# A first stage rebuilt around PSUM: the convolution, the samples and the GLA projections of a hybrid decoder step

## The reference

```python
h = rmsnorm(x, norm_mix)
p = h @ w_in                               # 1024 -> 9248 columns
qkv, z, b_a, a_a, q_b, k_b, v_b, r_b, lr, g_a, g_b = split(p)
xc = concat([conv_buf, qkv])               # 3 old rows ahead of the new ones
conv = sum(cw[i] * xc[i:i+T] for i in range(4))
new_buf = last 3 rows of xc
q_a, k_a, v_a = split(silu(conv))          # 8 heads of 128; q_a, k_a are l2-normalized
beta, g = sigmoid(b_a), -exp(a_log) * softplus(a_a + dt_bias)
o_a, S_a = gated_delta_net(S_a, q_a, k_a, v_a, g, beta)
lg = log_sigmoid(lr @ gla_gate_up + gla_gate_bias) / 16
o_b, S_b = gla(S_b, q_b / sqrt(128), k_b, v_b, lg)    # 4 heads, keys 128, values 256
merged = sigmoid(g_a) * (norm(o_a)*silu(z)) @ w_proj_a + sigmoid(g_b) * (norm(o_b)*silu(r_b)) @ w_proj_b
x = x + merged @ w_out
x = x + experts(rmsnorm(x, norm_ffn))      # 32 experts in 4 groups, 2 chosen per token
y = rmsnorm(x, norm_final)
```

## Time and profile before

| | us |
|---|---|
| Median of 3 runs (lowest, highest) | 1073.52 (1070.82, 1075.18) |
| Profiled execution | 1078.4 |
| its span | 1076.7 |
| Busy: PE, PEld, DVE, ACT, POOL | 928.6, 745.7, 442.7, 298.3, 304.9 |
| Mean granted clock of TensorE | 0.895 |

### The profile page before, as it was taken

One profiled execution on the slowest core, in us unless ns is written; L12 is line 12 of the kernel. 1 busy time (PEld: TensorE's weight loads), 2 busy tenths in 40 slices (PEclk: granted clock), 3 DMA queues, 4 the chain that ended last, 5 costly groups with the idle time before them and its releaser, 6 DMA issues. The chain is left out here.

```text
span 1076.7 us, 15504 instructions
## 1 busy us (share of the span) xinstructions
PE 928.6 (86%) x6446; PEld 745.7 (69%) x6446; DVE 442.7 (41%) x718; ACT 298.3 (28%) x602; POOL 304.9 (28%) x281
## 2 busy tenths in 40 slices
PE   4989877988899699968988999999769999889964
PEld 2888757988898698745558999999756455455521
DVE  5689874544313532153355632464142222102213
ACT  3454363231112334211036443432201111110102
POOL 8366446375341200034234301756000000000000
PEclk9999889998688698988868999999955999999996
DMA  9544006000002592300443554420190999999981
GB/s 252 174 141 128 1 1 169 1 1 1 2 1 79 152 299 79 118 0 1 154 163 87 157 157 157 156 79 1 59 422 8 394 420 419 419 420 419 419 370 47
DMA packets 97910, 175.71 MB, mean 163 GB/s; under 512 B 8964, under 2 KB 84324, under 8 KB 85493
## 3 DMA queue, kind: packets, MB, share of 16 engines
q1 hardware_dynamic: 97832, 174.62, 44.9%
HBM read 163.66 MB, written 10.95 MB: 162 GB/s over the span
## 5 line engine op out<-in xcount | busy, mean ns | idle before, releaser
L243 PE MATMUL ps<-rounded,rounded 128*128 128x304 f32 x640 | 201.4, 315 | 13.5 <-DVE rounded L231 9.5
L245 PE MATMUL ps<-rounded,rounded 128*128 128x304 f32 x640 | 195.9, 306 | 0.0
L244 PE MATMUL ps<-hL,rounded 128*128 128x304 f32 x512 | 157.9, 308 | 0.0
L243 PEld LDWEIGHTS ps<-rounded,rounded 128*128 128x128 f32 x640 | 123.5, 193 | 15.7 <-DVE rounded L231 9.7
L231 POOL TENSOR_TENSOR rounded<-ring,rounded 128x2048 fp32r<-128x2048 f32 x21 | 98.3, 4679 | 104.4 <-ACT rounded L225 104.4
L245 PEld LDWEIGHTS ps<-rounded,rounded 128*128 128x128 f32 x640 | 123.6, 193 | 0.0
L225 ACT ACTIVATE rounded<-ring 128x2048 fp32r<-128x2048 f32 x48 | 91.3, 1910 | 37.5 <-PE ps L245 16.0
L244 PEld LDWEIGHTS ps<-hL,rounded 128*128 128x128 f32 x512 | 99.7, 195 | 0.4 <-issue 0.2
L231 DVE TENSOR_TENSOR rounded<-ring,rounded 128x2048 fp32r<-128x2048 f32 x27 | 63.3, 2344 | 70.9 <-ACT rounded L225 70.2
L1904 DVE TENSOR_TENSOR arena<-arena,ps 128x512 f32<-128x512 f32 (+1 forms) x48 | 32.9, 685 | 123.3 <-PE ps L2022 123.3
L1952 PE MATMUL ps<-arena 128*128 128x128 f32 (+1 forms) x384 | 74.7, 328 | 2.5 <-DVE arena L1871 2.5
(11 more groups left out here) (334 smaller groups left out, 1602.4 us busy)
## 6 DMA issues: line engine op xcount, KB each, us to landing
ring<-in_w_in SPq DMA_DIRECT2D x36, 1024.0 KB, 5.7
ring<-in_expert_w_gate SPq DMA_DIRECT2D x32, 1024.0 KB, 14.4
ring<-in_expert_w_up SPq DMA_DIRECT2D x32, 1024.0 KB, 19.6
arena<-in_expert_w_down SPq DMA_DIRECT2D x32, 1024.0 KB, 17.6
arena<-in_state_gla SPq DMA_DIRECT2D x4, 1024.0 KB, 6.7
out_sg_s<-arena SPq DMA_DIRECT2D x4, 1024.0 KB, 4.2
ring<-in_w_proj_a SPq DMA_DIRECT2D x4, 1024.0 KB, 5.4
ring<-in_w_proj_b SPq DMA_DIRECT2D x4, 1024.0 KB, 5.1
```

The lines of the kernel that those rows point to most:

```text
L243: self.nc.tensor.matmul(self.psum[b][:, 0:NT], h[:, j, c], xh(j), start=(j == 0), stop=False)
L244: self.nc.tensor.matmul(self.psum[b][:, 0:NT], h[:, j, c], xl(j), start=False, stop=False)
L245: ins = self.nc.tensor.matmul(self.psum[b][:, 0:NT], lo[:, j, c], xh(j), start=False, stop=(j == KB - 1))
```

## The change

In the first stage:

- GpSimd prepares slot 0 alone, high part and low part, and takes all later low parts up to slot 19 except that of slot 1 (VectorE's). Its masks are built in pieces between them. The transfer of slot 0 goes out right after x, slot 1 ahead of the small columns.
- The high part of the activations moves from VectorE to ScalarE. Block 0 starts with the first piece of the activations that is ready.
- The low-rank product becomes 24 rounded matmuls and goes behind block 1, the gates' turns behind block 2, the log decays behind block 5.
- The convolution of the prompt reads PSUM where the block was made, in four shifted operations; the block's bank is freed by the convolution. There is no XC for the prompt.
- The samples of eight blocks are gathered in a PSUM bank (XS) beside their old rows, put there by a product with the identity for eight blocks at a time (`history`), and convolved together in seven operations (`sample_conv`). `new_buf` is collected by ScalarE.
- GLA's slots follow the convolution, values first (order of `WIN`). Twelve units of `unit_of_slot`, with the sums of squares, norms and turns of the delta heads spread between them by the table AFTER; the squares are ScalarE's, the inverse roots are written to PSUM. Then eight blocks of q_b and k_b, with the turns of the old rows between them.
- The results lie in ring slots 4 to 7 (VB, QKB) until the GLA stage has used them, and with them the two gate tables (UP, GB), loaded at the start of `delta`. From slot 20 on the ring is shifted by four (`slot`, `occupant`, `fills`), so that four slots are loaded during GLA and the next ones in `merge`.

The GLA stage keeps the log gates, the key turns and its loop. It waits for the delta stage's stores later than before: GpSimd at once, VectorE ahead of its first pair, ScalarE at its third exponents.

The core of the diff:

```diff
+def slot(n):
+    return (n if n < N_Z else n + 4) % SLOTS
+
+def occupant(n):
+    return max((m for m in range(n) if slot(m) == slot(n)), default=None)
...
+    def unit_of_slot(self, pe, n, c, b, HI):
+        pe.wait_ge(self.w_lo, n + 1)
+        hi, lo = (w.rearrange("p (j c) -> p j c", j=KB) for w in (HI[n % 3], self.LOW[:, slot(n), :]))
+        o = self.psum[b][0:L[c], 0:256]
+        for j in range(KB):
+            x, y = (h[:, j, T0[c]:T0[c] + L[c]] for h in (self.hH, self.hL))
+            self.nc.tensor.matmul(o, x, hi[:, j, :], start=(j == 0), stop=False)
+            self.nc.tensor.matmul(o, x, lo[:, j, :], start=False, stop=False)
+            ins = self.nc.tensor.matmul(o, y, hi[:, j, :], start=False, stop=(j == KB - 1))
+        ins.then_inc(self.unit_done, 1)
...
+    AFTER = {1: ("ss0",), 2: ("v0", "v1", "ss2"), 3: ("v2", "v3", "ss4"), 4: ("v4", "v5", "ss6"), 5: ("v6", "v7", "ss8"),
+             6: ("k0", "k1", "ss10"), 7: ("k2", "k3", "ss12"), 8: ("k4", "k5", "ss14"), 9: ("k6", "k7")}
...
     @block.gpsimd  (front)
+        k.arrived(pl, 0)
+        nc.gpsimd.tensor_copy(HI[0], k.ring[:, 0, :]).then_inc(k.w_hi, 1)
+        k.low_part(pl, nc.gpsimd, 0, HI)
...
+        pl.drain().then_inc(s["mask_ready"], 1)
+        k.low_part(pl, nc.gpsimd, 2, HI)
+        k.low_part(pl, nc.gpsimd, 3, HI)
         blocks(BLK, 16)
...
+        for n in range(8, N_Z):
+            k.low_part(pl, nc.gpsimd, n, HI)
...
     @block.scalar  (front)
+        for j in range(KB):
+            act.wait_ge(s["xT_done"], j + 1)
+            nc.scalar.activation(hH[:, j, :], psum[4 + j % 4][:, 0:NT], ACT.Copy, scale=nm[:, j:j + 1]).then_inc(s["hH_ready"], 1)
+        k.high_part(act, 2, HI)
...
         for b in range(NCB):
+            g = b // 8
+            if b == 2:
+                low_rank()
             if b == 3:
+                gates_by_token()
+            if b == 4:
+                gate_exps()
+            if b == 7:
                 decays()
...
+            nc.scalar.activation(XS[g][:, b % 8, :, 3:], psum[b % 4][:, TP:NT].rearrange("p (a r) -> p a r", r=TS), ACT.Copy).then_inc(s["xs_ready"], 1)
+            nc.scalar.activation(LAST[:, b, 0:3], psum[b % 4][:, TP - 3:TP], ACT.Copy).then_inc(s["tail_ready"], 1)
+            if b % 8 == 7:
+                act.wait_ge(s["xs_ready"], b + 1)
+                sample_tail(g)
+            if b % 2 and b // 2 + 3 <= N_VB + 2:
                 k.high_part(act, b // 2 + 3, HI)
             if b >= 2:
                 silu(b - 2)
+            if b in (10, 18):
+                sample_silu(b // 8 - 1)
...
+        def square(i):
+            b = KEYS_FIRST[i][1]
+            if i >= 2:
+                act.wait_ge(s["ssum_done"], i - 1)
...
+            nc.scalar.activation(SQ[:, i % 2, :], place(b), ACT.Square).then_inc(s["sq_ready"], 1)
+        def norm(i):
+            act.wait_ge(s["ssum_done"], i + 1)
+            p = psum[5 + 2 * (i % 2)][:, 0:NT]
+            link(nc.scalar.activation(RS[:, i % 2, :], p, ACT.Ln, bias=epsc))
+            nc.scalar.activation(p, RS[:, i % 2, :], ACT.Exp, scale=-0.5).then_inc(s["rs_ready"], 1)
...
     @block.vector  (front)
+        def sample_conv(g):
+            dve.wait_ge(s["last_ready"], g + 1)
...
+            link(nc.vector.tensor_tensor(acc, XS[g][:, :, :, 0:TS], weight(0), ALU.mult))
+            for r in range(1, CW):
+                link(nc.vector.tensor_tensor(tap, XS[g][:, :, :, r:r + TS], weight(r), ALU.mult))
+                ins = nc.vector.tensor_tensor(acc, tap, acc, ALU.add)
...
         for b in range(NCB):
-            dve.wait_ge(s["hist_ready"], b + 1)
-            if b >= 2:
-                dve.wait_ge(s["conv_silu"], b - 1)
-            x, o = XC[:, b % 3, :], CV[:, b % 2, 0:XW - 3]
-            link(nc.vector.tensor_scalar(o, x[:, 0:XW - 3], cw[:, 0, b:b + 1], None, ALU.mult))
+            dve.wait_ge(s["tail_ready"], b + 1)
+            if b >= 3:
+                dve.wait_ge(s["conv_silu"], b - 2)
+            x, o = psum[b % 4], CV[:, b % 3, :]
+            link(nc.vector.tensor_scalar(o, x[:, 0:TP], cw[:, 3, b:b + 1], None, ALU.mult))
             for r in range(1, CW):
-                ins = nc.vector.scalar_tensor_tensor(o, x[:, r:XW - 3 + r], cw[:, r, b:b + 1], o, ALU.mult, ALU.add)
+                ins = nc.vector.scalar_tensor_tensor(o[:, r:], x[:, 0:TP - r], cw[:, 3 - r, b:b + 1], o[:, r:], ALU.mult, ALU.add)
...
+            if b == 2:
+                gates_before()
+            if b == 4:
+                gates_after()
+            if b % 8 == 7:
+                sample_conv(b // 8)
...
     @block.tensor  (front)
         for b in range(NCB):
+            if b >= 4:
+                pe.wait_ge(s["conv_ready"], b - 3)
+            k.block_of_slot(pe, b // 2, b % 2, b % 4, HI, arrives=s["xT_evac"] if b == 0 else None)
...
+            if b == 1:
+                low_rank()
+                pe.wait_ge(s["sc_in"], 16)
                 pe.wait_ge(s["par_ready"], 1)
+                history(0)
+                history(1)
...
+            if b == 5:
+                log_decays()
+            if b == 11:
+                pe.wait_ge(s["acc_ready"], 1)
+                pe.wait_ge(s["last_ready"], 1)
+                history(2)
...
+        for u in range(NV):
+            q, c = divmod(u, 3)
+            n = N_VB + q
+            if u < 4:
+                pe.wait_ge(s["conv_ready"], 21 + u)
+            else:
+                pe.wait_ge(s["vb_ready"], u - 3)
+            k.unit_of_slot(pe, n, c, u % 4, HI)
+            for kind, i in extras(u):
...
+        for b in range(8):
+            pe.wait_ge(s["vb_ready"], NV) if b < 4 else pe.wait_ge(s["qkb_ready"], b - 3)
+            k.block_of_slot(pe, N_QB + b // 2, b % 2, b % 4, HI)
```

More of the change, by code:

```diff
@@ L64, in units, with fills @@
 def units(n):
-    return sum(3 if N_VB <= k < N_Z or k >= N_WO else 2 for k in range(n))
+    return sum(3 if N_VB <= k < N_QB or k >= N_WO else 2 for k in range(n))
+def slot(n):
+    return (n if n < N_Z else n + 4) % SLOTS
+def occupant(n):
+    return max((m for m in range(n) if slot(m) == slot(n)), default=None)
+def fills(n):
+    return sum(slot(m) == slot(n) for m in range(n + 1))
 def named(nc, stage, names):
@@ L198, in load_w @@
     def load_w(self, sp, n):
-        if n >= SLOTS:
-            sp.wait_ge(self.unit_done, units(n - SLOTS + 1))
+        if occupant(n) is not None:
+            sp.wait_ge(self.unit_done, units(occupant(n) + 1))
         if n < N_PA:
@@ new lines, in front @@
+    SC = k.carve(2432, CONV)
+    VT = k.carve(2432, 8 * NT, 8, NT)
+    HI = [k.carve_r(A1 + SW * p, SW) for p in range(3)]
+    CV = k.carve(14720, 3 * TP, 3, TP)
+    SQ = k.carve(15536, 2 * NT, 2, NT)
+    RS = k.carve(16144, 2 * NT, 2, NT)
+    XN = k.carve(17792, 3072, 3, D)
+    SCO = k.carve(17792, CONV)
+    CWR = k.carve(20864, 128)
+    wsm = k.carve(20992, KB * 48, KB, 48)
+    wsH, wsL = (k.carve_r(21376 + KB * 48 * p, KB * 48, KB, 48) for p in range(2))
+    smT = k.carve(22144, NT)
@@ L359, in _ @@
             blocks(GR[:, r, :], m)
+        k.low_part(pl, nc.gpsimd, 5, HI)
+        for r, m in ((3, 32), (4, 16)):
+            v = GR[:, r, :].rearrange("p (a h b) -> p a h b", h=2, b=m)
+            for h, src in ((0, SL), (1, U)):
+                half = src.rearrange("p (a h b) -> p a h b", h=2, b=m)
+                link(nc.gpsimd.tensor_copy(v[:, :, h, :], half[:, :, h, :]))
+            blocks(GR[:, r, :], m)
+        k.low_part(pl, nc.gpsimd, 6, HI)
         link(nc.gpsimd.tensor_tensor(GM[:, 0, :], U, BLK, ALU.mult))
@@ L577, in tr, with history @@
             return nc.tensor.transpose(out, in_, ident[0:n, 0:n])
+        def history(g):
+            for b in range(8 * g, 8 * g + 8):
+                ins = mm(XS[g][:, b % 8, :, 0:3], SC[0:24, 128 * b:128 * b + 128], ident[0:24, 0:24].rearrange("p (a r) -> p a r", r=3),
+                         start=True, stop=True)
+            ins.then_inc(s["hist_done"], 1)
         pe.wait_ge(s["ident_ready"], 1)
@@ L592, in _ @@
-        pe.wait_ge(s["xT_evac"], 8)
-        for j in range(KB):
-            for x in (hH, hL):
-                ins = mm(psum[7][0:48, 200:200 + NT], wsm[:, j, :], x[:, j, :].bitcast(F32),
-                         start=(j == 0 and x is hH), stop=(j == KB - 1 and x is hL))
-        ins.then_inc(s["lr_done"], 1)
-        pe.wait_ge(s["smT_ready"], 1)
-        for c in range(3):
-            tr(psum[6][0:L[c], 16 * c:16 * c + 16], smT[0:16, T0[c]:T0[c] + L[c]], 16).then_inc(s["small_done"], 1)
@@ L1122, in gla @@
     ss_in = (s["ss_in0"], s["ss_in1"])
-    HI = [k.carve_r(8576 + SW * p, SW) for p in range(3)]
     l3 = L[2]
@@ L1256, in _ @@
         link = Chain(dve, s["dve_c"])
-        for n in range(N_QB, N_Z - 1):
-            k.low_part(dve, nc.vector, n, HI)
         for c in range(3):
@@ L1695, in slot_filled @@
     def slot_filled(eng, v, n):
-        eng.wait_ge(slot_in[n], (v + 1) * 16 + (16 * (N_PRE // SLOTS) if n < SLOTS else 0))
```

(3 more changed lines are left out.)

497 lines of the change are left out of this document (239 added, 258 removed).

## The result

The changed kernel takes 1066.38 us (median of 13 runs, 1062.99 to 1075.31), the kernel before 1074.49 (13 runs); the ratio is 0.9928, 95% interval 0.9906 to 0.9949. By the ratio that is 7.7 us less (by the medians 8.1) where 30 were forecast, and outside the range of 1028 to 1062. The profiled execution is the slowest of the 13: 1075.31 us, span 1073.6, against 1078.4 and 1076.7 of before.

A forecast was written before the change was run, and what follows sets the result against it. Stages between barriers add up; the first was paced by VectorE's stalls beside GpSimd's low parts. 1078.4 + 39 (until delta's start) − 69 (GLA preamble) = 1048.4, factor 0.972; 1073.5 x 0.972 = 1043.5 us, range 1028 to 1062.

The forecast's parts named there:

- Low parts don't stop a convolution that reads PSUM: First stage: VectorE's operations with PSUM input stay near 0.5 us beside GpSimd's low parts, 2.0 a block against TensorE's 3.36.
- the pace from block 6 on: First stage, blocks 6 to 23: TensorE bounds, 60.5 us of blocks, history 1.2, restart at low clock 1.4, ending at 123.0.
- So they end near 22.4: Start of the first stage: the transposes of x pace themselves as before and end near 22.4 us.
- I take 58 for the gates, a wait of 7 (bounds 0 and 12): First stage, behind block 5: gates ready at 58 us, so TensorE waits 7 us before the log decay products.
- History 2.4: First stage, behind the low-rank product: history products for 16 blocks at 0.15 us each, 2.4 us, ending at 37.2.
- Projections and tail 53.8, query and key blocks 30.2: First stage after block 23: value units with sums and turns 53.8 us, to 176.8; query and key projections 30.2, to 207.0.
- the relay rival: First stage's tail: each pair of sums of squares costs 3 us that no unit covers, +21, 1064 us; chance 0.12.
- The preamble, bounds 12 to 19: Start of the GLA stage: first exponent product at 384.0 us instead of 452.90, 15 us after delta's end; −69 us.
- Sum: Whole kernel: 1078.4 + 39 − 69 = 1048.4 us profiled, factor 0.972, so 1043.5 us for the median.
- the lock: First stage: PSUM convolution and GpSimd exclude each other after all, 8.7 us a slot instead of 6.7; +24, 1067; chance 0.06.
- the clock case: First stage: new waits put TensorE at 1.2 GHz, 2.7 us more a block; 16 blocks give 1086; chance 0.06.
- that rival's 1029: First stage: gates never late and sums of squares find their inputs, preamble 2 us shorter; −45, 1029 us; chance 0.18.

The follow-up runs named there:

- the three edits: Changed kernel plus one table load ahead of the gate activations, slot 0's low part held until x is normalized, log decay sums moved later: 1047.81 us, ratio 0.9746.

## Why the prediction was wrong

- *Low parts don't stop a convolution that reads PSUM*: right, shown by undoing it (+17 us at delta's start, +22 in the time), and so is the pace from block 6 on: 18 blocks, a history and a restart in 65.7 us for 63.1. The Trainium skill states a cause for both signs, in "SBUF — State Buffer", section "Who interferes with whom": GpSimd shares one pair of SBUF ports with VectorE, under an exclusive lock, and an instruction of VectorE with at most one SBUF input, outside its two-port modes, stays off that pair. The trace agrees: 0.50 against up to 4.83 us for one multiply-add. One SBUF input did not protect the multiply from SBUF (up to 4.68 us for 0.36) or the normalization of x; whether those ran in a two-port mode, no row shows. The copy to SBUF that the other page, cited in the prediction, advises would have been the wrong way here, though its price for PSUM inputs is there: 0.14 us for the multiply of each block, near the estimate of 0.1.
- *"So they end near 22.4"*, with slot 0 that "GpSimd prepares ... during the wait for x", was the first failed step. I took GpSimd's new work as free because it is ready in time, and left out what it locks on VectorE, though I used that very lock two paragraphs later. 4.2 us in the profile; holding it back gave 5.8.
- *"I take 58 for the gates, a wait of 7 (bounds 0 and 12)"* was the largest miss, 14.95, outside its bounds. The count of ScalarE's queue had "two or three table loads". The profile before shows none within the gates, since the set with both functions was still active there; the change puts a Silu ahead of them. Five of the six loads, which one named load replaces, were 6.4 us of the 8, and the low clock behind the long wait cost the next 1.8. The Trainium skill, "ScalarE: Activation LUTs", section "Table sets: the hidden batching unit", gives a logarithm followed by an exponential as one load, since one set holds both. The trace differs: without a load of that set named ahead of them, six were made; with it, one.
- *History 2.4* measured 5.1. I took 0.15 for a product from transposes; it is two instructions of 0.12 at the high clock, 3.9 us for both groups, and the clock fell in them for the rest and for most of block 2 behind.
- *Projections and tail 53.8, query and key blocks 30.2*: 51.4 and 30.8, and 1.5 for the 2.0 of evacuation and barrier. No pair of sums cost time that the units don't cover, so the relay rival is out.
- *The preamble, bounds 12 to 19*: 22.9. I composed it of three spans of the earlier trace rows, cut from a stage in which TensorE was hot and the products were done long before. Bare, each chunk waits for products at the low clock (first 3.8 us for 2.3, then 9.6 for 6.7, then 7.9 for 6.1, and 1.5 of barrier).
- *Sum*: +21.3 up to block 23, −2.3 behind it and +7.8 in the preamble make 26.8 us, the difference between the forecast −30 and the −3.1 of the profiled executions. Two terms came out above their upper bounds, and the start had none. None of the rivals was it: the nearest in time, the relay (1064) and the lock (1067), are both refuted as I put them, so that they came near is chance, and so is the clock case refuted (0.93 over the whole first stage, 0.95 to 1.00 in its long windows). With the three edits, in which the gates are indeed never late, the kernel takes 1047.8 us, not that rival's 1029: history and preamble keep their price, and the first sum of squares still waits 2.2 us.

## What to carry to other kernels

Price an instruction that moves to another engine by what it locks and by what activation set it finds, not by its duration alone: here one wait, one table load and a later place for the log decays held 19.5 of the 23 us that were missing. When work is stripped from around a serial chain, take the chain's rows again at the low clock and with its waits, because those rows were measured under cover. And undo the part that you believe in: it was worth some 20 us, hidden in a net of 8 (with the copy that came back with it).

## What the runs showed that I had not expected

- One 48x8 operation of VectorE took 4.40 us beside a low part of 4.50, and a 48x72 one took 4.27 to 4.49 in four of the other versions: the lock can cost nearly a whole low part, however small the victim. In two versions no gate operation met one.
- The clock fell from 2.4 to 1.2 GHz within busy products of 16 rows and 1 row (423.55 us above), and in or behind the 32 short instructions of the history.
- Delta, unchanged, took 194 or 200 to 201 us by its granted clock: nearly as much as the net effect of this change. The GLA loop did the like, 99.1 to 99.9 us in seven profiles and 102.7 to 103.7 in three, at granted clocks of 0.84 to 0.85 and 0.80 to 0.81.
